# Expert blocks of a mixture-of-experts layer as pairs of 64-row sub-blocks side by side in the TensorE array, plain float32 on raw weights, row records in SBUF, two tables of sums

## Chip, cores and metric

One NeuronCore of one Trainium2 chip runs the whole program. The metric is the device time of one execution in microseconds (us). A matmul takes a stationary operand (here the transposed rows of the activations) and streams a moving operand (here the weights) past it.

## The reference, cut to what matters

`x` is 2048 rows of 1024 float32. The first half of the layer (adaLN, attention, pooling, output projection) and the router are untouched by the change in what they compute. What matters is the mixture of experts:

```
scores = sigmoid(h2 @ w_router)                      # (2048, 128)
eidx   = top 8 experts of each row (group-limited);  wts = normalised scores * 2.5
routed[t] = sum over its 8 experts e of  wts * ((silu(h2[t] @ w_gate_e[e]) * (h2[t] @ w_up_e[e])) @ w_down_e[e])
shared    = (silu(h2 @ w_sh_gate) * (h2 @ w_sh_up)) @ w_sh_down
out = rmsnorm(x1 + gate2 * (routed + shared), final_g)
# w_gate_e, w_up_e: (128, 1024, 256) float32;  w_down_e: (128, 256, 1024) float32: 3 MiB an expert
```

With the inputs given, the router sends between 26 and 410 rows to an expert, 16384 in all. In blocks of 128 rows that makes 198 blocks, and 16 more for the shared expert: 214. In sub-blocks of 64 rows it makes 315, and 32 for the shared expert: 347, or 174 pairs.

## The kernel before

**Stages.** First the conditioning vector is multiplied by `ada_w`, then a loop over 16 tiles of 128 rows does the first half of the layer and the router. It stores `x1` to `acc_tab` and `h2` to `h2_tab` in HBM, and for each routed row a record (row number, weight) into `rec_tab` in HBM, ordered by expert (eight indirect DMAs of POOL a tile, L449). Then the vector engine works out which block belongs to which expert (a chain of small instructions from L819 to L865), the tables go through HBM into one partition (`row_tab`), and the expert stage begins. A last stage reads `acc_tab`, normalises and stores `out`.

**Expert stage.** A loop over blocks of 128 rows, unrolled 8 times on each engine, run `nblk+1` times. For each block the engines do this:
- POOL (L484 to L492, and `load_rec`, L475 to L478): gather the 128 rows of `h2` of block b+4 by the indices in `rec`, an SBUF tile of 8 slots (indirect DMA, L461), scatter-add the 128 result rows of the block before into `acc_tab` (indirect DMA with add, L492), and load the records of block b+6 from HBM (L478). Before the gather it waits until all record loads issued so far have landed: `g.wait_ge(s["rec_ld"], b * 16 + 16 * (AHEAD + 2))` counts the one issued in the iteration before. Before the scatter-add it waits for the one before it (`added`).
- PE: 24 matmuls of gate and up (`parts`, L1068 to L1070, operands XR and WS), 8 transposes of the next block's rows (`transposes`, L956), 12 matmuls of down with two transposes of the hidden layer (L1097) between them. Every product is made of three: the operands are split into a high and a low part in the reduced format float32r, and high*high, high*low and low*high are summed.
- ACT: silu (L608), the high parts of rows (L590), of the hidden layer (L616) and, once per expert, of the 6144 columns of weights (`upper`, L586).
- DVE: the low parts of the same (`rows_lower`, L894; L921; `lower`, L887), the product of gate and up (L908), and the scaling of the results (L917), which waits for `added`.
- SP: the weights of an expert into one of two slots of `RAW`, in two transfers of 1 MiB for gate and up and one for down, in runs of 1 KiB per row of gate and up; a slot is free when the split has read it.

The order of the work is written out by hand and kept by semaphores; no scheduler moves anything.

## Time and profile before

| | us |
|---|---|
| median of three executions (3545.75 to 3561.34) | 3558.13 |
| span of the profiled execution, first to last instruction | 3472.9 |
| what lies around that span, against the median | 85.2 |
| expert stage in that span, first L1068 to last L1070 | 985.3 to 3417.4 |

The page's second part cuts the span into 40 slices. Its first 2 are loads and conditioning, up to about slice 11 the tile loop, from there to slice 39 the expert stage. A float32 matmul stands in the profile as two records, a float32r one or a transpose as one. The duration of a record includes its latency, so that the pitch of a run of them is found from the starts, or from (length of the run less one record) divided by (count less one).

### The profile page before, as it was taken

To read this page: it belongs to the slowest core of one execution; us is meant where nothing else is said; L and a number is where in the kernel's file an instruction comes from. 1 tells how busy PE (TensorE), PEld (TensorE's weight loads), DVE (VectorE), ACT (ScalarE), POOL (GpSimd) and SP (SyncE) were. 2 spreads that over 40 slices of the span, in tenths; PEclk is the share of its full clock that TensorE was granted. 3 is DMA by queue.
4 is the path that set the end of the run, shared out by engine and by line. 5 is a ranking of instruction groups with operands and counts; after the bars stand their busy time and mean duration, and the time that the engine had idled before them with its cause. 6 is when DMAs were issued, how large, how long until landed. Compare 5 with 4: busy or idle time off the path is not lost.

```text
span 3472.9 us, 61999 instructions
## 1 busy us (share of the span) xinstructions
PE 2951.9 (85%) x13151; PEld 2180.6 (63%) x13152; DVE 2164.1 (62%) x3443; ACT 1706.3 (49%) x2435; POOL 925.5 (27%) x794
## 2 busy tenths in 40 slices
PE   6699999999469989888798888888888888998883
PEld 2355555555358877776676767676767667776662
DVE  1146666666643665667676766666766675667774
ACT  0133333333133654656565655556556565656565
POOL 0001111111223333232333333333332323333331
PEclk9899999999779999999899999999999999999896
DMA  9501111111175887989998999899989998899997
GB/s 368 163 25 49 49 48 36 49 36 43 67 182 122 239 228 208 269 260 259 289 295 252 290 281 274 258 271 285 288 259 265 265 293 232 247 266 280 294 275 249
DMA packets 415300, 730.08 MB, mean 210 GB/s; under 512 B 31521, under 2 KB 297377, under 8 KB 414754
## 3 DMA queue, kind: packets, MB, share of 16 engines
q1 hardware_dynamic: 341314, 500.17, 42.5%
q0 software_dynamic: 73824, 228.47, 28.6%
q14 instruction: 149, 1.22, 0.1%
q8 instruction: 13, 0.21, 0.0%
HBM read 587.37 MB, written 141.19 MB: 210 GB/s over the span
## 4 chain that ended last, share of the span: by engine, by line
DMA 45%; PE 22%; issue 12%; DVE 8%; POOL 7%; POOLq 4%; ACT 2%; DVEq 0%; SPq 0%; ACTq 0%
DMA rec<-rec_tab 42%; PE PB L986 8%; POOL arena L461 3%; POOL acc_tab L492 3%; POOLq L476 3%; PE PB L951 2%; PE PB L1068 2%; PE PB L1070 2%; PE PB L1069 2%; DMA arena<-in_ada_b 1%; PE PB L1045 1%; PE PB L956 1%; DMA acc_tab<-arena,rec 1%; PE PB L970 1%; PE PB L1011 1%
## 5 line engine op out<-in xcount | busy, mean ns | idle before, releaser
L887 DVE TENSOR_TENSOR WS<-RAW,WS (+1 forms) x774 | 900.8, 1219 | 127.3 <-ACT WS L586 125.3
L586 ACT CAST WS<-RAW (+1 forms) x774 | 759.5, 1052 | 153.2 <-DMA RAW<-in_w_up_e 99.6
L1068 PE MATMUL PB<-WS,XR 128*128 x1720 | 685.6, 399 | 52.2 <-issue 46.6
L461 POOL DMA_INDIRECT arena<-h_tab,rec x219 | 255.3, 1166 | 1574.7 <-DMA rec<-rec_tab 1381.1
L1070 PE MATMUL PB<-WS,XR 128*128 x1720 | 674.7, 392 | 0.0
L1069 PE MATMUL PB<-WS,XR 128*128 x1720 | 674.0, 392 | 0.0
L917 DVE SCALAR_TENSOR_TENSOR arena<-PB,rec,G 128x512 f32<-128x512 f32 x430 | 302.5, 745 | 383.7 <-DMA acc_tab<-arena,rec 336.5
L1068 PE MATMUL PB<-WS,HR 128*128 x860 | 402.9, 468 | 154.1 <-DVE HR L921 153.0
L492 POOL DMA_INDIRECT acc_tab<-arena,rec x215 | 402.5, 1872 | 93.3 <-issue 68.4
L1068 PEld LDWEIGHTS PB<-WS,XR 128*128 128x128 f32 x1720 | 327.6, 190 | 158.7 <-issue 91.8
L1069 PEld LDWEIGHTS PB<-WS,XR 128*128 128x128 f32 x1720 | 326.7, 190 | 66.1
L1070 PEld LDWEIGHTS PB<-WS,XR 128*128 128x128 f32 x1720 | 325.4, 189 | 67.6
L1070 PE MATMUL PB<-WS,HR 128*128 x860 | 363.4, 423 | 0.0
L1069 PE MATMUL PB<-WS,HR 128*128 x860 | 361.6, 420 | 0.0
L956 PE MATMUL PB<-cst,arena 128*128 128x128 f32 x1984 | 265.4, 278 | 97.3 <-DVE arena L814 53.1
L449 POOL DMA_INDIRECT rec_tab<-recs,posi x128 | 124.6, 973 | 795.5 <-DVE recs L748 754.8
L956 PEld LDWEIGHTS PB<-cst,arena 128*128 128x128 f32 x1984 | 235.8, 143 | 138.2 <-DVE arena L814 48.4
L894 DVE TENSOR_TENSOR XR<-PB,XR 128x512 fp32r<-128x512 f32 x432 | 277.6, 684 | 65.0 <-ACT XR L590 64.8
L608 ACT ACT_TABLE_LOAD x215 | 275.8, 1283 | 74.4 <-issue 70.5
L1068 PEld LDWEIGHTS PB<-WS,HR 128*128 128x128 f32 x860 | 176.4, 205 | 193.0 <-issue 169.4
L986 PE MATMUL PB<-arena 128*128 128x512 f32 (+1 forms) x768 | 293.7, 544 | 1.5 <-ACT arena L515 1.2
L590 ACT ACTIVATE XR<-PB 128x512 fp32r<-128x512 f32 x432 | 234.6, 595 | 98.3 <-PE PB L956 98.3
(233 smaller groups left out, 2982.6 us busy)
## 6 DMA issues: line engine op xcount, KB each, us to landing
RAW<-in_w_gate_e SPq DMA_DIRECT2D x128, 1024.0 KB
RAW<-in_w_up_e SPq DMA_DIRECT2D x128, 1024.0 KB
RAW<-in_w_down_e SPq DMA_DIRECT2D x128, 1024.0 KB, 8.6
arena<-in_ada_w SPq DMA_DIRECT2D x12, 2048.0 KB, 14.3
arena<-in_x SPq DMA_DIRECT2D x32, 512.0 KB, 3.6
h_tab<-arena SPq DMA_DIRECT2D x17, 512.0 KB, 2.9
acc_tab<-arena SPq DMA_DIRECT2D x16, 512.0 KB, 2.6
out<-fa SPq DMA_DIRECT2D x16, 512.0 KB, 4.7
```

The source lines that it names most:

```text
L461: g.indirect_dma_start(xg[n % AHEAD], None, h2_tab, bass.IndirectOffsetOnAxis(ap=rec[:, n % UNROLL, 0:1], axis=0)).then_inc(s[f"xg_r{n % A ...
L492: g.indirect_dma_start(acc_tab, bass.IndirectOffsetOnAxis(ap=rec[:, (n - 1) % UNROLL, 0:1], axis=0), ys[(n - 1) % 2], None, compute_op=ALU ...
L586: nc.scalar.copy(to, of).then_inc(s["a_hig" if k < 4 else "a_hid"], 1)
L608: A_(eg, B[7][:, 0:F], ACT.Silu).then_inc(s["eg_done"], 1)
L887: last = V.tensor_tensor(lo, raw, hi, ALU.subtract)
L894: V.tensor_tensor(xl[:, 4 * n:4 * n + 4, :], B[2 + n].rearrange("p (a b) -> p a b", a=4), xhf[:, 4 * n:4 * n + 4, :], ALU.subtract).then_i ...
L917: last = V.scalar_tensor_tensor(out=ys[(n - 1) % 2][:, c * 512:(c + 1) * 512], in0=B[4 + c], scalar=recf[:, (n - 1) % UNROLL, 1:2], in1=G2 ...
L956: last = tr(B[banks[k // 4]][:, (k % 4) * P:(k % 4 + 1) * P], src[:, k * P:(k + 1) * P], ident)
L986: last = mm(B[4 + n][:, 0:w], xT[:, k, :], w_in[:, k, n * 512:n * 512 + w], start=(k == 0), stop=(k == KD - 1))
L1068: mm(bank, hi[:, k, :], w(k, 0), start=(k == 0), stop=False)
L1069: mm(bank, hi[:, k, :], w(k, EW), start=False, stop=False)
L1070: last = mm(bank, lo[:, k, :], w(k, 0), start=False, stop=(k == K - 1))
```

## The change

It does seven things together.
1. Units of two 64-row sub-blocks, A and B, replace blocks of 128 rows. A's results come out in PSUM partitions 0 to 63 and B's in 64 to 127: each matmul has a stationary operand of 128 rows by 64 columns, and A's and B's alternate. The two sub-blocks of a unit may belong to two experts. 174 units instead of 214 blocks.
2. Plain float32 matmuls on the weights as loaded. The three float32r products and the splits of weights, rows and hidden layer are gone. A reads its weights in the ring where they were loaded; for B, DVE copies gate and up (4096 columns, `gu_copy`) and ACT copies down (2048 columns, `down_copy`) of each unit to `WBG` (two buffers) and `WBD` (one).
3. A ring of four slots for weights instead of two, and loads in runs of 8 KiB per partition (`(p k)` instead of `(k p)`); the columns of `h2` and of the hidden layer are permuted to match, in the instruction that writes them (last axis stepped by 128).
4. The records of all units are read from `rec_tab` once, by four indirect DMAs, transposed by PE and kept in SBUF (`RI`, `RW`); DVE copies two columns of them a unit into `rec`. The load of records in POOL's loop is gone.
5. Two tables of sums: A adds to the first half of `acc_tab` and B to the second, which SP fills with zeros during the tile loop (16 stores of 512 KB). The last stage reads both and DVE adds them.
6. Padding rows are not gathered (an index out of bounds); they are still scattered.
7. The block tables go to one partition by 7 small matmuls instead of through HBM, and POOL clears the row buffers (128x4096) once.

The core of the diff:

```diff
-SLOTS = 2
+SLOTS = 4
+SUB = 64
@@ SP, tile loop
+                if ok(i):
+                    sp.dma_start(acc_tab[bass.ds(i * P + (T + P), P), :], zeros).then_inc(s["z_acc"], 16)
@@ SP, loads
+            def gate_up(l, e):
+                at = (l + 3) % SLOTS * EW
+                sp.dma_start(RING[:, at:at + HALF], g.rearrange("a (p k) n -> p (a k n)", p=P)).then_inc(s["w_g"], 16)
+                sp.dma_start(RING[:, at + HALF:at + GUW], u.rearrange("a (p k) n -> p (a k n)", p=P)).then_inc(s["w_u"], 16)
@@ SP, last stage
                 sp.dma_start(fa[:, lo:hi, :], acc_tab[lo * P:hi * P, :].rearrange("(t p) n -> p t n", p=P)).then_inc(s[f"f_in{n}"], 16)
+                sp.dma_start(fb[:, lo:hi, :], acc_tab[lo * P + T + P:hi * P + T + P, :].rearrange("(t p) n -> p t n", p=P)).then_inc(s[f"f_ib{n}"], 16)
@@ POOL
+            g.wait_ge(s["p_wo"], NT)
+            g.memset(arena[:, 34816:34816 + AHEAD * D], 0.0).then_inc(s["z_pool"], 1)
+            g.wait_ge(s["e_off"], 1)
+            g.wait_ge(s["st_rec"], 16 * TOPK * NT)
+            for c in range(4):
+                g.indirect_dma_start(RF[:, c].rearrange("p r a -> p (r a)"), None, rec_sub,
+                                     bass.IndirectOffsetOnAxis(ap=recb[:, c:c + 1], axis=0)).then_inc(s["e_rec"], 16)
...
                             g.wait_ge(s["xg_used"], b + 1)
-                            g.wait_ge(s["rec_ld"], b * 16 + 16 * (AHEAD + 2))
+                            g.wait_ge(s["v_rec"], b + (AHEAD + 1))
                             gather(n + AHEAD)
                             g.wait_ge(s["y_v"], b + 2)
                             g.wait_ge(s["added"], b * 16 + 32)
-                            g.indirect_dma_start(acc_tab, bass.IndirectOffsetOnAxis(ap=rec[:, (n - 1) % UNROLL, 0:1], axis=0),
-                                                 ys[(n - 1) % 2], None, compute_op=ALU.add).then_inc(s["added"], 16)
-                            load_rec(b + (AHEAD + 2), (n + AHEAD + 2) % UNROLL)
+                            g.indirect_dma_start(acc_tab, bass.IndirectOffsetOnAxis(ap=rec[:, n, 1:2], axis=0),
+                                                 ys[n % 2], None, compute_op=ALU.add).then_inc(s["added"], 16)
@@ ACT, loop
                             act.wait_ge(s["gu_done"], b + 2)
+                            silu()
+                            act.wait_ge(s["xg_used"], b + 3)
                             rows_upper()
                             act.wait_ge(s["y_done"], b + 1)
+                            hidden_T()
+                            act.wait_ge(s["w_d"], need)
+                            down_copy(RING[:, bass.ds(act.snap(at + GUW), HALF)])
@@ DVE, tile loop
-                    V.tensor_tensor(h2, h2, B2, ALU.add).then_inc(s["v_h2"], 1)
+                    V.tensor_tensor(h2.rearrange("t (k p) -> t p k", k=KD), tmpf.rearrange("t (p k) -> t p k", k=KD),
+                                    B2.rearrange("t (p k) -> t p k", k=KD), ALU.add).then_inc(s["v_h2"], 1)
@@ DVE, loop
+                            v.wait_ge(s["eg_done"], b + 2)
+                            gated()
+                            v.wait_ge(s["xg_used"], b + 3)
+                            rows_lower()
                             v.wait_ge(s["y_done"], b + 1)
                             v.wait_ge(s["added"], b * 16 + 16)
...
+                                last_ = V.scalar_tensor_tensor(out=ys[n % 2][:, c * 512:(c + 1) * 512], in0=B[4 + c], scalar=RW[:, bass.ds(b, 1)],
+                                                               in1=G2[:, c * 512:(c + 1) * 512], op0=ALU.mult, op1=ALU.mult)
...
+                            V.tensor_copy(rec[:, (n + 5) % UNROLL, :], pair[:, bass.ds(b + 5, 1), :].rearrange("p n a -> p (n a)")).then_inc(s["v_rec"], 1)
+                            v.wait_ge(s["w_g"], need)
+                            v.wait_ge(s["w_u"], need)
+                            gu_copy(n + 1, RING[:, bass.ds(at, GUW)])
@@ PE
+            def gate_up(n, wa):
+                for k in range(KD):
+                    mm(B[7][0:SUB, :], xTm[:, k, 0:SUB], wa(k), start=(k == 0), stop=(k == KD - 1))
+                    last = mm(B[7][SUB:P, :], xTm[:, k, SUB:P], WBG[n % 2][:, k], start=(k == 0), stop=(k == KD - 1))
+                last.then_inc(s["gu_done"], 1)
+            def down(c, wa):
+                for k in range(2):
+                    mm(B[4 + c][0:SUB, :], hT[:, k, 0:SUB], wa(k), start=(k == 0), stop=(k == 1))
+                    last = mm(B[4 + c][SUB:P, :], hT[:, k, SUB:P], WBD[:, k * D + c * 512:k * D + (c + 1) * 512], start=(k == 0), stop=(k == 1))
+                return last
```

Two places of the instruction order. First PE, in one iteration of the expert loop of the kernel before, from the end of gate and up to the end of down (WS are the split weights, HR the split hidden layer, cst holds the identity for transposes):

```order
L1070 MATMUL PB<-WS_50,XR_51 128x512
...
L956 MATMUL PB<-cst,arena 128x128 [waits xg_r3]
L956 MATMUL PB<-cst,arena 128x128 x7
...
L1068 REGISTER_ALU [waits v_spd]
...
L1068 MATMUL PB<-WS_50,HR_52 128x512
L1069 ISA
L1069 MATMUL PB<-WS_50,HR_52 128x512
L1070 MATMUL PB<-WS_50,HR_52 128x512
...
L1097 MATMUL PB<-cst,arena 128x128 [waits h_ready]
L1097 MATMUL PB<-cst,arena 128x128
```

The same place of the changed kernel (L1089 and L1090 are A and B of gate and up, L1096 and L1097 those of down, L977 and L1102 the transposes; the 64 is the number of PSUM partitions written):

```order
L1089 ISA [waits xgT_v,xgT_a,v_cg]
L1089 MATMUL PB<-arena 64x512
L1090 MATMUL PB<-arena 64x512
...
L977 MATMUL PB<-cst,arena 128x128 [waits xg_r3]
L977 MATMUL PB<-cst,arena 128x128 x7
...
L1096 ISA [waits a_cd,hT_a,y_v]
L1096 MATMUL PB<-arena 64x512
L1097 MATMUL PB<-arena 64x512
...
L1102 MATMUL PB<-cst,arena 128x128 [waits h_ready]
L1102 MATMUL PB<-cst,arena 128x128
```

The order of the four pieces is unchanged; the triples of full width are now pairs of half width (8 pairs for gate and up, 4 for down), and the waits on the splits (`v_spd`, `hT_sb`) are replaced by waits on the copies for B (`v_cg`, `a_cd`).

Second POOL, one iteration of its loop before:

```order
L486 ISA [waits xg_used]
L461 DMA arena<-h2_tab,rec 128x1024 [waits rec_ld]
L488 REGISTER_ALU
L490 REGISTER_ALU [waits y_v]
L492 DMA acc_tab<-arena,rec 2176x1024 [waits added]
...
L476 TENSOR_LOAD cst
...
L478 DMA rec<-rec_tab 128x2
```

And in the changed kernel:

```order
L506 REGISTER_ALU [waits xg_used]
L477 DMA arena<-h2_tab,rec 128x1024 [waits v_rec]
L508 REGISTER_ALU
L509 ISA [waits y_v]
L511 DMA acc_tab<-arena,rec 4352x1024 [waits added]
```

The gather no longer waits for a DMA that the same loop issued one iteration earlier; the scatter-add keeps its waits. The third place, DVE, one iteration of the loop of the changed kernel (before it the weights were split here once per expert, in six instructions of 1024 columns):

```order
L892 TENSOR_TENSOR arena<-arena,PB 128x128x2 [waits eg_done]
L916 REGISTER_ALU
L889 COPY arena<-PB 128x512 [waits xg_used]
L918 REGISTER_ALU
L919 ISA [waits y_done]
L922 ISA [waits added]
L922 SCALAR_TENSOR_TENSOR arena<-PB,RW_50,G2 128x512 x2
L925 ISA
L925 COPY rec<-RI_49 128x2
L886 ISA [waits w_g,w_u]
L886 COPY arena<-arena 128x4096
```

Every unit now has one copy of 4096 columns, behind the scaling, and it waits for the weights of the unit three ahead.

## Rows read from the trace of the kernel before

**Rows 1.** The page: span, and the chain that ended last.
```profile
span 3472.9 us, 61999 instructions
...
DMA rec<-rec_tab 42%; PE PB L986 8%; POOL arena L461 3%; POOL acc_tab L492 3%; POOLq L476 3%; PE PB L951 2%; PE PB L1068 2%; PE PB L1070 2%; PE PB L1069 2%; DMA arena<-in_ada_b 1%; PE PB L1045 1%; PE PB L956 1%; DMA acc_tab<-arena,rec 1%; PE PB L970 1%; PE PB L1011 1%
```
**Rows 2.** Busy time by stage; last columns TensorE clock, DMA share, GB/s.
```profile
170.00:914.00 744.00, 682.88 (x2966) 402.11 (x2964) 478.61 (x1174) 247.55 (x493) 108.68 (x112) 0.96 0.12 43
985.00:1160.00 175.00, 173.83 (x838) 142.92 (x839) 78.75 (x122) 71.09 (x106) 55.45 (x50) 0.99 0.64 163
1160.00:3417.00 2257.00, 1972.43 (x9054) 1576.38 (x9052) 1518.70 (x1936) 1326.61 (x1737) 730.38 (x591) 0.95 0.91 265
```
**Rows 3.** POOL in order of time, in the expert stage.
```profile
2318.76 0.99 POOL L461 DMA_INDIRECT arena<-h_tab,rec  x1 [8.87 <-DMA rec<-rec_tab]
2320.05 1.62 POOL L492 DMA_INDIRECT acc_tab<-arena,rec  x1 [0.30 <-issue]
2321.08 1.23 POOL L478 DMA_DIRECT2D rec<-rec_tab  x1
2330.77 0.98 POOL L461 DMA_INDIRECT arena<-h_tab,rec  x1 [8.46 <-DMA rec<-rec_tab]
```
**Rows 4.** DMA issues with median us to landing: stretch 1000 to 1160, then 3100 to 3200.
```profile
q0 software_dynamic: 5120, 16.80, 48.1%
...
acc_tab<-arena,rec POOLq DMA_INDIRECT x17, 6.7
...
acc_tab<-arena,rec POOLq DMA_INDIRECT x9, 9.4
```
**Rows 5.** PE in order of time: one block without a wait, from down to down.
```profile
3404.83 0.47 PE L1068 MATMUL PB<-WS,HR 128*128 x1
...
3413.35 1.04 PE L956 MATMUL PB<-cst,arena 128*128 128x128 f32 x8
3414.15 0.48 PE L1068 MATMUL PB<-WS,HR 128*128 x1
```
**Rows 6.** PE in order of time in the tile loop; stationary size after the operands.
```profile
500.21 1.59 PE L970 MATMUL PB<-arena 64*64 64x128 f32 x32
...
523.43 2.05 PE L1011 MATMUL PB<-arena 128*128 128x128 f32 x16 [0.65 <-ACT arena L539]
525.41 1.09 PE L1022 MATMUL PB<-arena 128*64 128x256 f32 x8
526.44 1.16 PE L1026 MATMUL PB<-arena,poolw 128*128 128x128 f32 x8
...
899.69 13.97 PE L1045 MATMUL PB<-arena 128*128 128x512 f32 x32 [1.31 <-DVE arena L767]
```
**Rows 7.** Groups by line: count, then busy us, mean ns.
```profile
L887 DVE TENSOR_TENSOR WS<-RAW,WS x768 | 893.8, 1219 | 109.8 <-ACT WS L586 107.8 <-issue 0.2
L586 ACT CAST WS<-RAW x768 | 753.6, 1052 | 106.7 <-DMA RAW<-in_w_up_e 99.6
...
L1045 PE MATMUL PB<-arena 128*128 128x512 f32 x512 | 223.5, 594 | 12.1 <-DVE arena L767 12.1
...
L917 DVE SCALAR_TENSOR_TENSOR arena<-PB,rec,G 128x512 f32<-128x512 f32 x430 | 302.5, 745 | 383.7 <-DMA acc_tab<-arena,rec 336.5 <-PE PB L1070 47.1
...
L774 DVE TENSOR_TENSOR arena<-arena,rbias 128x128 f32<-128x128 f32 x16 | 4.7, 294 | 0.6
L772 DVE TENSOR_SCALAR arena<-arena 128x128 f32<-128x128 f32 x16 | 3.5, 218 | 4.1 <-ACT arena L546 4.1
...
L435 POOL MEMSET arena<- 128x1024 int32 x1 | 1.0, 984 | 0.0
```
**Rows 8.** The hardware DMA queue in the last stage (3427 to 3473): packets, MB, share.
```profile
q1 hardware_dynamic: 4432, 16.78, 90.8%
```
**Rows 9.** Between tile loop and experts: POOL's last record store and first gather.
```profile
958.94 0.96 POOL L449 DMA_INDIRECT rec_tab<-recs,posi  x1 [0.30 <-issue]
961.98 1.00 POOL L461 DMA_INDIRECT arena<-h_tab,rec  x1 [2.08 <-DVE offi L865]
```

559 lines of the change are left out of this document (283 added, 276 removed).

## The prediction

> **What bounds the kernel now.** I read the page first. The chain that ended last is 42% loads of records from `rec_tab`, a transfer of 1 KB [rows 1]; PE's matmuls of the expert stage stand in it with 2% a line, although PE is busy 1972 us of the 2257 us between 1160 and 3417 [rows 2]. So I asked for POOL in order of time. A record load is issued at 2321.08 for 1.23 us, then POOL sits idle 8.46 us for it before it may gather; from gather to gather 12.01 us pass [rows 3]. The loop is paced by a latency: gather, scatter-add and load are issued (about 3.5 us), then the load, behind the scatter-add in the same queue, has to land. The expert stage runs from 985.3 to 3417.4, 2432 us for 215 iterations, 11.3 us each. What PE would need without waits shows in one block at the end: from 3404.83 to 3414.15, 9.32 us from down to down [rows 5]. That is 36 float32r matmuls at 0.228 and 10 transposes at 0.11. The DMA engines are the near second, 0.91 busy in that stage [rows 2]. So PE, DMA and the record chain lie within 2 us of each other, and taking away one alone would give at most 2 us a block.
>
> **The change part by part.**
>
> *PE, a unit.* A float32 record of 512 columns comes every (13.97 - 0.59) / 31 = 0.43 us [rows 6, 7], and a matmul is two of them: 0.86 us, against three float32r records, 0.68 us, before. On its own that would be dearer by a quarter. What decides is whether A and B, each 64 columns wide in the array, run at the same time. The trace has this very shape: L1022, stationary 128*64, its output first in one half of the PSUM partitions and then in the other, 8 records of 256 columns. One after another they would need 8 x 0.216 = 1.73 us until the next matmul may start; the next, L1026, starts 1.03 us after the first [rows 6]. Four steps of 0.216 make 0.86, so they ran two at a time, and 0.17 us are left over for changing the array's shape in and out. L970 says the same: 32 records of 128 columns, 3.45 us if serial, took 1.59. I therefore price a pair of matmuls at one: 0.86 us. L1026's own 8 records take 1.16 us where 8 of L1011's (16 in 2.05) would take 1.1 or less, and L1022 starts late behind L1011 by about as much, so I take 0.35 us for each change in and out, between 0.17 and 0.5.
>
> The unit has 8 pairs of gate and up (6.88), 4 pairs of down (3.44), 10 transposes at 0.11 (1.1) and two changes in and out, round the 8 transposes and round the 2 (0.7): 12.12 us. The bounds are 11.8 and 12.6. The Trainium skill, TensorEngine Tiling (Array Packing), section Key Properties, states that changing the tiling mode drains the TensorE. The trace agrees: the drain is the 0.17 us left over above; no figure stands on that page.
>
> *The expert stage.* 174 x 12.12 + 6.9 (one gate and up ahead of the loop) = 2116 us, against 2432: **-316**. The blocks get 0.8 us longer than they were, and there are 41 fewer. The whole gain is that count: 174 units against 215 iterations, since half-size sub-blocks waste fewer padding rows.
>
> *What must hide behind 12.1 us.* DVE: one product and one copy of half the width and the full width of a scaling, two scalings at 0.745, and the copy of 4096 columns. Its price is not in the trace. L887 takes 1.219 us for 1024 columns and L774 0.294 for 128, so 1.03 ns a column from two SBUF sources; L772, with one source, takes 0.218 for 128, which is about half of that a column [rows 7]. So the copy costs between 2.3 (taken) and 4.4 us, and DVE 5.1 to 7.4 us a unit. It ends before the next gate and up does; the result of the silu is then waited for only behind 8 transposes and half of down. ACT: 2048 columns at 1.03 ns (L586 [rows 7]) 2.1 us, under 5 with the rest and its table load. The single buffer for B's down is refilled while PE spends 6.9 us on gate and up. POOL: its chain is now scatter-add to scatter-add, each waiting for the one before to land: 6.7 us with the DMA engines 0.64 busy, 9.4 with them nearly full [rows 2, 4], plus 0.3. Under 12.1 in either case; the record load and its wait are off it. This is the cover for it: 2.4 us. DMA: the weights are 402.7 MB; at the rate of the last stage, 16.78 MB in 90.8% of 46 us, 402 GB/s [rows 8], they need 1002 us of all engines. Gather and scatter-add take 48.1% of 160 us for 16.80 MB, 16.5 blocks: 4.7 us a block [rows 4], 811 us for 174, less where padding is skipped. 1813 of 2116 us, 0.86; past the 16 units of the shared expert, whose weights are there, 0.90. Before it was 0.91 with two slots, and four will smooth more.
>
> *Between the stages.* POOL issued its last record store until 959.9 [rows 9]. Then come a memset of 4096 columns (4 x 0.98 [rows 7]), four record gathers at the spacing of 1.3 us, their landing, a few small copies and transposes (about 5 us), four row gathers and the first transposes. By these I reach 985, where the first matmul stood before. The table's round trip through HBM, which was waited for, is gone: **0**, between -6 and +6.
>
> *Last stage.* Twice as much is read: 8.39 MB more at 402 GB/s is 21 us. The stage was 90.8% full, so a little fits into its holes: **+18**, between +12 and +25. DVE's 16 additions at 1.2 us lie beside the loads.
>
> *Tile loop.* The 16 stores of zeros fall where the DMA share is 0.12 [rows 2]. The permuted write of `h2` has no row; it costs nothing if a stepped write runs at the speed of a plain one, and at worst doubles a 1.2 us instruction in 16 tiles, 20 us, in a loop in which PE is busy 0.92: **+3**, between 0 and +20.
>
> Sum: -316 + 0 + 18 + 3 = -295, span 3178. The profiled execution's span is 3472.9 and the median 3558.13; I carry the 85.2 us between them over unchanged and get **3263 us**. All bounds on one side would give 3193 or 3377; since they won't all fall there, the forecast's own range is 3205 to 3345.
>
> **The rivals.**
>
> *A. Pairs overlap only in part (slower, 0.08).* The gain is 295 us, or 1.70 us a unit; spread on 24 pair steps of 0.43 that is 0.07. So from a step of 0.50 on the kernel is slower. Fully serial steps give 174 x 10.3 = 1792 us more, 5055. Against it stands L1022 with four steps for eight records; for it, that L1022 is a short burst of 256 columns with no long DVE copy beside it, and that its two halves are issued one after the other, not alternating for every step. The Trainium skill, TensorE: Matmul & The Clock Gate, section Part 3, gives 2.38 for three column tiles, 0.79 of ideal; if two tiles reached 0.79, a step would be 0.54, and the time 3263 + 174 x 24 x 0.11 = 3722. By that rule; the trace has 1.73 / 0.86, the ideal 2, once the change of shape is taken off.
>
> *B. The scatter-add takes the place of the record load (0.10).* If the copy of 4096 columns keeps POOL from preparing its transfers, POOL's period is 9.4 + 0.3 + 2.3 to 4.4, that is 12.0 to 14.1 us. At the lower end it costs nothing, in the middle (13.0) 174 x 0.9 = 157, 3420; only from 13.8 on is it slower (0.02 of the 0.10). No row has such a copy beside a POOL issue. The Trainium skill, SBUF — State Buffer, describes just this as the "DVE blocks DMA" trap: a one-source float32 copy on DVE locks GpSimd out of the shared port while descriptors are to be written. Nothing in this trace shows it, as DVE's long operations here have two sources.
>
> *C. Weights come late (0.07).* At 0.90 of the DMA engines, a run of experts with under 64 rows asks 3 MiB, 7.5 us, for half a unit, 6 us. DVE's copy looks three units ahead, which eats the ring. 0.5 to 1 us a unit gives 3350 to 3437. Against it: an expert has 16 us of PE on average.
>
> *D. Better than priced (0.04).* Changes of shape that cost nothing and a step of 0.41 would give 10.9 us a unit, 3263 - 174 x 1.2 = 3054; half of that is 3160.
>
> *E. Gains and losses cancel (0.03)*, a unit at 13.8 by several small waits.
>
> **How the numbers follow.** Forecast 0.68, A 0.08, B 0.10, C 0.07, D 0.04, E 0.03. Faster by over 0.5% (about what a measurement of this kernel tells from no change): 0.68 + 0.08 + 0.07 + 0.04 = 0.87. Within 0.5%: 0.03. Slower: 0.08 + 0.02 = 0.10. The range from 3205 to 3420 leaves out A, D, E and the upper part of B, 0.2 together.
>
> **What the changed profile would show.** The expert stage lasts about 2116 us and PE passes a unit in 12.1. Two records of L1089 and L1090 start within some 0.02 us of each other and the next two 0.43 later; if they start 0.43 apart from one another, A is true. No wait on a record load remains. The scatter-add lands in under 10 us and its issue takes under 2; if the issue grows to 3 or more, B has its cause. PE's waits for DVE are those on `v_cg` (copy or weights late, C) or on `h_ready`. TensorE's clock is near 1.0 in the whole stage, where it was 0.95. The copy of 4096 columns takes 2.3 us or up to 4.4. The last stage lasts about 73 us instead of 56. I am wrong most easily in the unit: each 0.1 us in it is 17 us.

## The result, and the profile after

The changed kernel takes 3196.51 us (3194.67 to 3198.84, four executions) against 3551.94 us for the kernel before (3545.64 to 3561.34, four executions). The ratio is 0.8991, its 95% interval 0.897 to 0.9012. The forecast was 3263 us with a range from 3205 to 3420. It was right in the direction and in the length of the changed kernel's span, but 66 us too high as a time, and the time lies 8.5 us below the range. The step that failed is the last one, the 85.2 us carried over from the profiled execution to the median.

The page of the changed kernel: its span, and the chain that ended last by engine and by line.

```profile
span 3192.6 us, 48012 instructions
...
PE 65%; DMA 2%; DVE 1%; issue 0%; SPq 0%; POOL 0%; ACT 0%; DVEq 0%; POOLq 0%; ACTq 0%
PE PB L1089 37%; PE PB L1096 20%; PE PB L977 6%; PE PB L1102 2%; DMA arena<-in_w_up_e 1%; DMA arena<-acc_tab 1%; PE PB L1090 1%; DVE arena L954 0%; DVE arena L940 0%; PE PB L1097 0%; DMA acc_tab<-arena,rec 0%; DMA arena<-h_tab,rec 0%; DMA arena<-rec_tab,recb 0%; SPq L446 0%; POOL arena L488 0%
```

Where [rows 1] had 42% of the chain on the load of records, it now runs through PE's own matmuls, A's of gate and up (L1089) and A's of down (L1096). The execution took 3194.67 us and its span is 3192.6: 2.1 us lie outside the span.

The changed kernel by stage; the columns are those of [rows 2].

```profile
170.00:914.00 744.00, 661.78 (x2928) 387.60 (x2927) 477.88 (x1138) 247.20 (x493) 103.46 (x107) 0.97 0.16 54
...
1200.00:3120.00 1920.00, 1902.21 (x9192) 685.84 (x9190) 789.92 (x954) 501.12 (x636) 587.59 (x318) 1.00 0.87 282
3120.00:3193.00 73.00, 0.00 (x0) 0.00 (x0) 41.70 (x57) 31.71 (x52) 0.00 (x0) 0.50 0.87 346
```

In the expert stage PE is busy 1902 of 1920 us at a granted clock of 1.00, and the DMA engines 0.87. Of the 18 us that are left, 8.8 lie behind its end (3111.2), and 9.0 are one wait. There the weights came late. DVE's copy waited 14.08 us for them. The product of gate and up (L892) stands behind that copy in DVE's order, so it came late and kept PE waiting:

```profile
3032.09 2.29 DVE L886 COPY arena<-arena 128x4096 f32 x1 [14.08 <-DMA arena<-in_w_up_e]
...
3034.30 0.59 DVE L892 TENSOR_TENSOR arena<-arena,PB 128x256 f32<-128x256 f32 x1
...
3034.95 0.69 PE L1102 MATMUL PB<-cst,arena 128*128 128x128 f32 x2 [9.02 <-DVE arena L892]
```

PE of the changed kernel in order of time, from the end of gate and up of one unit to the start of the next one's (L1089 is A's gate and up, L1090 B's, L977 the 8 transposes of rows, L1096 and L1097 down of A and B, L1102 the 2 transposes of the hidden layer).

```profile
2302.84 0.59 PE L1089 MATMUL PB<-arena 128*64 x1
2302.85 0.59 PE L1090 MATMUL PB<-arena 128*64 128x512 f32 x1
2303.37 1.09 PE L977 MATMUL PB<-cst,arena 128*128 128x128 f32 x8
2304.39 0.64 PE L1096 MATMUL PB<-arena 128*64 x1
2304.40 0.64 PE L1097 MATMUL PB<-arena 128*64 128x512 f32 x1
...
2305.73 0.59 PE L1096 MATMUL PB<-arena 128*64 x1
...
2306.26 0.44 PE L1102 MATMUL PB<-cst,arena 128*128 128x128 f32 x2
2306.63 0.64 PE L1096 MATMUL PB<-arena 128*64 x1
...
2308.39 0.59 PE L1089 MATMUL PB<-arena 128*64 x1
2308.40 0.59 PE L1090 MATMUL PB<-arena 128*64 128x512 f32 x1
2308.82 0.59 PE L1089 MATMUL PB<-arena 128*64 x1
```

A's record and B's start 0.01 us apart, and the next two 0.43 later. So the halves of the array run at the same time, and a pair costs what one matmul costs. What the change of the array's shape costs shows in the starts: from 2302.85 to 2303.37 is 0.52 where 0.43 would do, from 2303.37 to 2304.39 is 1.02 where 8 transposes at 0.11 would need 0.88, and the first pair of down takes 0.48. In and out cost 0.09 + 0.14 + 0.05 = 0.28 us; round the 2 transposes of the hidden layer it is as much.

The costliest groups of the changed kernel.

```profile
L511 POOL DMA_INDIRECT acc_tab<-arena,rec x174 | 459.6, 2641 | 1414.0 <-DVE arena L922 1268.2
...
L886 DVE COPY arena<-arena 128x4096 f32 (+1 forms) x177 | 405.4, 2290 | 54.3 <-DMA arena<-in_w_up_e 53.3
```

POOL now waits for DVE's results (L922), which wait for PE. That is the wait of an engine with time to spare. The wait of a scatter-add for the one before it is 77.6 us in all. The copy of 4096 columns takes 2.29 us, as taken (2.3).

**The sum, term by term, in that execution.** The expert stage ran from 1001.6 to 3111.2, that is 2109.6 us, where 2116 was forecast, against 2432.1 before (985.3 to 3417.4): -322.5. It began 16.3 us later (+3 was forecast up to there). What follows it took 81.4 us against 55.5: +25.9, where +18 was forecast. The sum is -280.3 against the forecast -295, a span of 3192.6 against 3178. So the span was forecast to 0.5%. The rest of the miss is the last step, the 85.2 us.

### The profile page after: what moved, and what is told of

The parts are those of the page before. It is cut to its first block, busy times and chain, and to the rows that moved or that the text cites. A ratio compares the mean times of both kernels' runs of the same rounds, so it can differ in the third digit from the quotient of the medians.

```text
span 3192.6 us, 48012 instructions
## 1 busy us (share of the span) xinstructions
PE 2898.3 (91%) x13408; PEld 1210.9 (38%) x13409; DVE 1463.7 (46%) x2449; ACT 853.0 (27%) x1285; POOL 788.2 (25%) x493
## 4 chain that ended last, share of the span: by engine, by line
PE 65%; DMA 2%; DVE 1%; issue 0%; SPq 0%; POOL 0%; ACT 0%; DVEq 0%; POOLq 0%; ACTq 0%
PE PB L1089 37%; PE PB L1096 20%; PE PB L977 6%; PE PB L1102 2%; DMA arena<-in_w_up_e 1%; DMA arena<-acc_tab 1%; PE PB L1090 1%; DVE arena L954 0%; DVE arena L940 0%; PE PB L1097 0%; DMA acc_tab<-arena,rec 0%; DMA arena<-h_tab,rec 0%; DMA arena<-rec_tab,recb 0%; SPq L446 0%; POOL arena L488 0%
## 5 line engine op out<-in xcount | busy, mean ns | idle before, releaser
L1089 PE MATMUL PB<-arena 128*64 (+1 forms) x2800 | 1231.9, 593 | 2.1 <-issue 1.3
L1090 PE MATMUL PB<-arena 128*64 128x512 f32 x2800 | 1231.9, 593 | 0.0
L511 POOL DMA_INDIRECT acc_tab<-arena,rec x174 | 459.6, 2641 | 1414.0 <-DVE arena L922 1268.2
L1089 PEld LDWEIGHTS PB<-arena 128*64 128x64 f32 x2800 | 384.0, 137 | 802.7 <-issue 802.7
L1096 PE MATMUL PB<-arena 128*64 x1392 | 673.5, 606 | 0.0
L1097 PE MATMUL PB<-arena 128*64 128x512 f32 x1392 | 673.5, 606 | 0.0
L922 DVE SCALAR_TENSOR_TENSOR arena<-PB,RW,G 128x512 f32<-128x512 f32 x348 | 245.3, 746 | 644.2 <-PE PB L1097 610.7
L886 DVE COPY arena<-arena 128x4096 f32 (+1 forms) x177 | 405.4, 2290 | 54.3 <-DMA arena<-in_w_up_e 53.3
L1090 PEld LDWEIGHTS PB<-arena 128*64 128x64 f32 x2800 | 384.0, 137 | 0.0
L892 DVE TENSOR_TENSOR arena<-arena,PB 128x256 f32<-128x256 f32 x175 | 106.2, 607 | 546.2 <-ACT arena L594 544.5
L603 ACT COPY arena<-arena 128x2048 f32 (+1 forms) x175 | 330.9, 1891 | 0.0
L977 PE MATMUL PB<-cst,arena 128*128 128x128 f32 x1664 | 231.3, 283 | 64.5 <-DVE arena L824 36.5
L594 ACT ACTIVATE arena<-PB 128x256 f32<-128x256 f32 x175 | 67.2, 384 | 826.3 <-PE PB L1090 727.7
L977 PEld LDWEIGHTS PB<-cst,arena 128*128 128x128 f32 x1664 | 182.8, 143 | 219.6 <-issue 158.9
L1096 PEld LDWEIGHTS PB<-arena 128*64 128x64 f32 x1392 | 162.1, 136 | 257.9 <-issue 257.9
L1066 PE MATMUL PB<-arena 128*128 128x512 f32 x512 | 236.9, 623 | 9.7 <-ACT arena L571 7.0
L600 ACT ACTIVATE arena<-PB 128x256 f32<-128x256 f32 x175 | 67.2, 384 | 622.9 <-PE PB L1097 622.9
L477 POOL DMA_INDIRECT arena<-h_tab,rec x178 | 193.8, 1089 | 62.5 <-issue 54.1
L1007 PEld LDWEIGHTS PB<-arena 128*128 128x128 f32 x768 | 145.2, 191 | 131.5 <-issue 120.1
L1097 PEld LDWEIGHTS PB<-arena 128*64 128x64 f32 x1392 | 162.1, 136 | 0.0
```

What stands on the lines that cost most here:

```text
L477: g.indirect_dma_start(xg[n % AHEAD], None, h2_tab, bass.IndirectOffsetOnAxis(ap=rec[:, n % UNROLL, 0:1], axis=0), bounds_check=T - 1, oob ...
L511: g.indirect_dma_start(acc_tab, bass.IndirectOffsetOnAxis(ap=rec[:, n, 1:2], axis=0), ys[n % 2], None, compute_op=ALU.add).then_inc(s["add ...
L603: nc.scalar.copy(WBD, src).then_inc(s["a_cd"], 1)
L886: V.tensor_copy(WBGf[n % 2], src).then_inc(s["v_cg"], 1)
L922: last_ = V.scalar_tensor_tensor(out=ys[n % 2][:, c * 512:(c + 1) * 512], in0=B[4 + c], scalar=RW[:, bass.ds(b, 1)], in1=G2[:, c * 512:(c ...
L977: last = tr(B[banks[k // 4]][:, (k % 4) * P:(k % 4 + 1) * P], src[:, k * P:(k + 1) * P], ident)
```

## The experiments

**The kernel before, again.** No edit.

> The kernel before, unchanged, profiled and timed again. The forecast carried 85.2 us over that lay between the span of before's profiled execution (3472.9) and its median (3558.13); in the changed kernel only 2.1 us lie outside the span (3194.67 against 3192.6). Theory 1: the execution of before that was profiled was a fast one, and other executions have an expert stage that is longer by some 80 us, because its pace is a transfer's latency, which differs from chip to chip or from execution to execution; then the spans here follow the times to within 3 us, and where the profiled span differs from 3473 the whole difference lies in the expert stage, in the time that a record load takes to land (about 0.4 us more than the 7.7 of the first trace). Theory 2: something outside the first and last instruction costs before 85 us and the changed kernel nothing; then the profiled span is near 3473 again with a time near 3550.

3495.6 us (3490.26 to 3504.01, ten executions) beside 3499.72 in 13 more executions of the same kernel, ratio 0.9994 (0.9974 to 1.0013). The profiled execution took 3490.94 with a span of 3489.3. So there are no 85 us outside the span, only 1.6, and this kernel took some 50 us less than when it was timed first. What differed was still open.

**The record load awaited one iteration later**, in the kernel before:

```diff
-                g.dma_start(rec[:, slot, :], rec_tab[bass.ds(off, P), :]).then_inc(s["rec_ld"], 16)
+                g.dma_start(rec[:, slot, :], rec_tab[bass.ds(off, P), :]).then_inc(s[f"rec_l{slot % 2}"], 16)
-                            g.wait_ge(s["rec_ld"], b * 16 + 16 * (AHEAD + 2))
+                            g.wait_ge(s[f"rec_l{n % 2}"], (q * (UNROLL // 2) + ((n + AHEAD) // 2 + 1)) * 16)
```

> The kernel before, in which POOL waits before a gather only for the records of the block that it gathers (issued two iterations earlier, on one of two semaphores), not for the load issued one iteration earlier. Theory 1 (the record load paces the loop): the iteration falls from 11.3-11.7 us to the next bound, the DMA engines or the scatter-add that waits for the one before it (9.4 us landing and its issue), about 10.3 us, so 215 us less, near 3330. Theory 2 (the DMA engines, 0.91 busy, are the real bound and the wait only stands where they show): under 50 us less, 3500 or more.

3329.49 us (3318.51 to 3338.35), ratio 0.9533 (0.9484 to 0.9583), as theory 1 had it. POOL's wait ahead of the gather (L461), in this kernel:

```profile
L461 POOL DMA_INDIRECT arena<-h_tab,rec x219: 941/992/4492, 957.9 to 3256.7; - x110
its engine sat idle before it (us, times) until:
  issue: 70.7, 213
```

The 1381 us for which the gather waited for records are gone, and the expert stage lasts 2280 us, 10.6 us a block instead of 11.4 (2451 us) for the kernel before in the same set. The latency paced the loop, as the prediction read it, and taking it away is worth 0.8 us a block, within the 2 us that the text allowed. What paces it next is no single thing: the DMA engines are 0.96 busy from 1160 to 3256, and POOL's scatter-add now waits 845 us in all for the one before it. Half of the change's gain could be had by moving one wait. Two more sets gave 3330.08 and 3328.59, ratios 0.9528 and 0.9547.

**A copy of two columns** instead of B's 4096, in the changed kernel; B then multiplies by stale weights.

```diff
-                            gu_copy(n + 1, RING[:, bass.ds(at, GUW)])
+                            V.tensor_copy(WBGf[(n + 1) % 2][:, 0:2], RING[:, bass.ds(at, 2)]).then_inc(s["v_cg"], 1)
```

> The changed kernel with DVE's copy of 4096 columns in the loop cut to 2 columns; B of a unit then multiplies by stale weights. Theory 1 (the copy is hidden, and what it lengthens is POOL's issue of the scatter-add): time within 3 us of 3196, the issue of the scatter-add falls from a mean of 2.64 us to 1.6 to 1.9. Theory 2 (the issue is longer for another reason, such as the second table or DMA queues): the issue stays at 2.6.

3177.28 us in one execution, 19 below the changed kernel as timed first. That was not the copy. The 19 us lie ahead of the expert stage, which begins at 984.8 instead of 1001.6 and lasts 2110.5 us against 2109.6 with the copy, and the changed kernel as it is gave 3177.69 in a later set (below). So the copy costs nothing that these times show. It does show in the scatter-add's issue (L511) and its landing; here, and in that later unchanged run:

```profile
L511 POOL DMA_INDIRECT acc_tab<-arena,rec x174: 1572/1581/1626, 1011.7 to 3097.9; - x174
...
DMA to landing us min/median/max: 5.9/6.6/10.3
```

```profile
L511 POOL DMA_INDIRECT acc_tab<-arena,rec x174: 1577/2797/2807, 1008.6 to 3097.9; - x174
...
  DVE arena L922: 1337.6, 165
...
  DMA acc_tab<-arena,rec: 8.6, 1
...
DMA to landing us min/median/max: 6.4/7.8/11.9
```

The issue takes 2.80 us with the copy and 1.58 without, so rival B's cause is real, up to 1.2 us a unit. Its effect on the time is not, since POOL sat idle 1338 us for DVE's results in that run and 8.6 us for a scatter-add. With the record load put back (below), POOL's order in time shifts, and the copy falls beside the gather's issue: there the gather's takes 2.45 us (at 2299.49, the copy at 2299.53) where it takes 1.04 without the copy beside it, and the scatter-add's 1.64. The Trainium skill, SBUF — State Buffer, "SBUF: two separate sides", describes such a wait as the "DVE blocks DMA" trap (GpSimd locked out of the shared port while DVE copies float32). The trace agrees with the longer issue; no run here shows the port.

**All of A's matmuls ahead of all of B's**, in the changed kernel:

```diff
                 for k in range(KD):
                     mm(B[7][0:SUB, :], xTm[:, k, 0:SUB], wa(k), start=(k == 0), stop=(k == KD - 1))
+                for k in range(KD):
                     last = mm(B[7][SUB:P, :], xTm[:, k, SUB:P], WBG[n % 2][:, k], start=(k == 0), stop=(k == KD - 1))
```

It is the same for down.

> The changed kernel with all matmuls of A before all of B, in gate and up (8 and 8) and in each half of down (2 and 2), the same work. Theory 1 (the array runs two column halves at once only if both are near each other in PE's queue): gate and up run one after the other, 6.9 us more, the halves of down perhaps too, up to 3.4 more; a unit of 19 to 22 us, time 4400 to 5000. Theory 2 (the two halves are independent streams however they are ordered, as the 8 records of two halves in the tile loop of before suggest): still 3196.

4075.7 us in one execution, between the theories. PE of this kernel in order of time (L1089 is A's gate and up, L1091 B's):

```profile
2306.46 5.74 PE L1089 MATMUL PB<-arena 128*64 x13
2311.62 0.64 PE L1091 MATMUL PB<-arena 128*64 128x512 f32 x1
...
2312.90 0.59 PE L1089 MATMUL PB<-arena 128*64 x1
2312.95 5.74 PE L1091 MATMUL PB<-arena 128*64 128x512 f32 x13
```

Of A's 16 records 12 run alone. From the thirteenth on B's start beside them, so that 4 of B's 16 are hidden and 12 run alone. That is 28 steps instead of 16, 12 x 0.43 = 5.2 us a unit, or 898 us for 174; the difference to the span of the changed kernel in the third set (below) is 4073.6 - 3176.5 = 897. In down, with 4 records each, everything is hidden. So here a record of B started while three of A's that were issued ahead of it had yet to start, but not while more had. It is the order of issue, A and B close to each other, that makes the pair cost one.

**The changed kernel, again.** No edit.

> The changed kernel once more, unchanged, beside the others. In its first profile PE passed a tile of the tile loop every 48.7 us and the expert stage began at 1001.6 us; in the runs with a two-column copy and with A's matmuls ahead of B's, which have the same tile loop word for word, a tile took 47.2 us and the stage began at 984.8 and 982.0. Theory 1: the difference belongs to the execution, not to the kernel (another pattern of half-speed stretches of TensorE in the tile loop); then this kernel shows 3174 to 3182 here, with the expert stage beginning near 984 and lasting 2110. Theory 2: the copy of 4096 columns, or the stores of zeros, slows the tile loop; then it shows 3194 to 3199 again. The kernel before should stand between 3477 and 3561, as it has so far, and in all runs the time outside the span is about 2 us.

3197.56 us (3194.62 to 3203.03) beside 3556.56 (3534.3 to 3572.01) for the kernel before. That is theory 2's number, but not for its reason: this set ran on another chip than the four runs before it, and there both kernels stood where they had been timed first. From here on I call these times the upper band (3534 to 3572 us for the kernel before, 3195 to 3203 for the changed one), and those of the first experiments, which the changed kernel joins below with 3174 to 3179, the lower band (3477 to 3512).

**One change of shape a unit**, in the changed kernel: the 8 transposes of rows behind the first half of down, directly ahead of the 2 of the hidden layer.

```diff
-                            m = n + 2
-                            pe.wait_ge(s[f"xg_r{m % AHEAD}"], (q * (UNROLL // AHEAD) + (m // AHEAD + 1)) * 16)
-                            transposes((2, 3), xg[m % AHEAD], "xg_used")
...
                             down(0, down_a(0))
+                            m = n + 2
+                            pe.wait_ge(s[f"xg_r{m % AHEAD}"], (q * (UNROLL // AHEAD) + (m // AHEAD + 1)) * 16)
+                            transposes((2, 3), xg[m % AHEAD], "xg_used")
                             pe.wait_ge(s["h_ready"], b + 2)
                             hidden_T()
```

> In the changed kernel PE enters and leaves the shape of 128 by 64 tiles twice in a unit: round the 8 transposes of rows and round the 2 of the hidden layer. Here the 8 transposes are moved behind the first half of down, directly ahead of the 2, so that it does so once. In the trace the starts around the 8 transposes leave 0.14 us behind them, those around the 2 leave 0.15 ahead and 0.15 behind, beyond 0.43 a record pair and 0.11 a transpose. Theory 1: what is left over is the price of the change of shape and nothing hides behind it; one change in and out is 0.30 us, 174 units give 52 us less, a ratio near 0.984, and a unit of 11.7 us. Theory 2: the DMA engines, 0.87 busy in this stage, are the next bound, and weights come late for units with few rows; then under half of it shows, 0 to 25 us, with PE's waits for DVE's copy growing. Theory 3: the rows' transposes now end 1.7 us later and the copies of them keep the next gate and up waiting; 0.2 to 0.5 us a unit more, 3230 to 3280.

3147.26 us (3143.25 to 3149.73) beside 3197.56: 50.3 us less where 52 were expected. PE of this kernel in order of time:

```profile
2304.16 0.59 PE L1090 MATMUL PB<-arena 128*64 128x512 f32 x1
2304.58 0.59 PE L1096 MATMUL PB<-arena 128*64 x1
...
2305.87 0.59 PE L1097 MATMUL PB<-arena 128*64 128x512 f32 x1
2306.39 1.09 PE L977 MATMUL PB<-cst,arena 128*128 128x128 f32 x8
2307.32 0.38 PE L1102 MATMUL PB<-cst,arena 128*128 128x128 f32 x2
2307.64 0.65 PE L1096 MATMUL PB<-arena 128*64 x1
...
2309.41 0.59 PE L1090 MATMUL PB<-arena 128*64 128x512 f32 x1
```

From gate and up (2304.16) to the next one's (2309.41) it is 5.25 us, against 5.55 in the changed kernel (2302.85 to 2308.40). The stage went from 2112 to 2061 us. The rows did not come late, and the weights only in the same place as in the changed kernel (one wait of 10.2 us of PE, 10.6 there). In the set with the fourth run of the kernel before, it gave 3126.13 (3123.97 to 3129.54), ratio 0.8949 (0.8904 to 0.8994), as was expected of it there:

> The changed kernel with one change of the array's shape a unit instead of two, beside the others: 3147 beside 3197 in the upper band. In the lower band 50 us less than 3177, that is 3122 to 3132, as the saving lies in the expert stage alone.

It is the best version measured.

**A plain write of `h2`**, in the changed kernel (the experts multiply rows of the weights in another order, and in this first run the router too, so that it makes 177 units):

```diff
-                    V.tensor_tensor(h2.rearrange("t (k p) -> t p k", k=KD), tmpf.rearrange("t (p k) -> t p k", k=KD),
-                                    B2.rearrange("t (p k) -> t p k", k=KD), ALU.add).then_inc(s["v_h2"], 1)
+                    V.tensor_tensor(h2, tmpf, B2, ALU.add).then_inc(s["v_h2"], 1)
```

> The changed kernel with h2 written in plain order instead of permuted (the products of the experts are then of other rows of the weights, so the routed part is not the reference's; all sizes and counts stay the same). The stepped write took 1.94 us against 1.22 for the plain one in the kernel before. Theory 1: DVE is on the path of the tile loop there, so 16 x 0.72 = 11.5 us are gained, a ratio of 0.9964 against the unchanged one. Theory 2: PE's order covers it, as PE is 0.9 busy in the loop; within 3 us, and L740 alone is shorter.

3278.37 us (3272.59 to 3286.26), 81 more. Both theories fell. Three more units are 36 us. The rest lay in the tile loop, in which the write is an instruction of 1.2 us: most tiles took 51.4 to 54.3 us instead of 48.8, and the stage began at 1049.3 instead of 1003.4. A shorter instruction had gone with a longer loop. So the run was done again with the router's weights in plain order as well (`"(k p) n -> p k n"` in their load), which makes 174 units.

> The plain write of h2 again, with the router's weights in plain order too, so that the router sends the same rows to the same experts and there are 174 units (the run before had 177); the experts still multiply rows of the weights in another order, so the routed part is not the reference's. The first one passed a tile in 51.4 to 54.3 us against 48.8, with PE waiting up to 4.2 us ahead of the scores and its clock at half behind it. Theory 1: that is what the shorter write sets off in the order of DVE, ACT and PE, and it comes again: tiles of 51 to 54 us, 3230 to 3245. Theory 2: it was of that execution or of those data; then the expected 11 us less, a ratio of 0.9964 against the unchanged one. If the set runs where before stands in the lower band, the tile may be 47.2 us or less in both.

3172.99 us (3172.6 to 3180.81) beside 3177.69 (3173.76 to 3178.93), where the kernel before stood at 3501.54: 5 us less by the medians, with ranges that overlap, and no slow loop. Most of those 5 us do not lie in the tile loop. Its expert stage begins at 980.5, that of the changed kernel in the same set at 981.2, and the rest of the difference lies in the expert stage (2109 against 2114 us), which the write is no part of. A tile takes 47.2 us (by the starts of the second to the fourteenth), but so it does with the stepped write in the run with A's matmuls ahead of B's. Within what these runs resolve, the shorter write gains nothing. Once more, in another set, one execution gave 3180.66:

> The changed kernel with the plain write of h2 and of the router's weights (same rows to the same experts; the routed part is not the reference's). In the lower band it passed a tile in 47.0 us and gave 3173 beside 3178, a gain of 5 where 11 were expected. In the upper band, theory 1: tiles of 51 to 54 us as in the first run of the plain write there, 3230 to 3245, since that chip puts TensorE's clock down inside the tile. Theory 2: about 48.8 us or less, 3185 to 3200, and the first run owed its tiles to its other data.

The upper band did not turn up for it, so its question stays open.

**The old record load put back** into the changed kernel's loop, to a tile that nobody reads:

```diff
+            def load_spare(slot):
+                g.dma_start(spare[:, slot, :], rec_tab[slot * P:(slot + 1) * P, :]).then_inc(s["rec_ld"], 16)
...
+                            g.wait_ge(s["rec_ld"], b * 16 + 16)
                             gather(n + AHEAD)
...
+                            load_spare(n)
```

> The changed kernel with the old record load put back into POOL's loop: 1 KB from the table of records to a spare tile, issued behind the scatter-add and waited for ahead of the next gather, as before the change; nobody uses what it loads. Theory 1: the chain of gather, scatter-add, load and its landing (1.04 + 2.8 + 1.2 us of issue and 7.7 to 8.1 us until it has landed, 12.7 to 13.1 us) is longer than PE's 12.0 us a unit, so it sets the pace: 0.8 to 1.2 us a unit, 140 to 210 us more, about 3320 to 3400. The change needed the records in SBUF for its gain. Theory 2: with 174 units instead of 215 blocks and the queue shorter, the landing falls to 6 to 7 us and hides; within 20 us of the unchanged one.

3311.23 us in one execution, 114 more, with the expert stage at 2224 us, 12.8 a unit; expected were 140 to 210. The record load landed after 9.2 us in the median. The chain that ended last in this kernel:

```profile
DMA 36%; PE 19%; POOL 8%; issue 5%; POOLq 1%; DVE 1%; SPq 0%; ACT 0%; DVEq 0%; ACTq 0%
DMA spare<-rec_tab 34%; PE PB L1097 11%; PE PB L1104 6%; POOL acc_tab L517 4%; POOL arena L478 3%; PE PB L985 2%; DMA arena<-h_tab,rec 1%; DMA arena<-acc_tab 1%; PE PB L1110 1%; DVE arena L962 0%; DVE arena L948 0%; PE PB L1098 0%; POOLq L512 0%; POOLq L259 0%; POOLq L509 0%
```

Without the records in SBUF, a third of the change's gain would be lost to the same latency.

**Both kernels in a third set, and the late record wait with them.** No new edits.

> The kernel before once more, for a third profile. Its executions have stood at 3477 to 3512 us in one set of runs and at 3534 to 3572 in two others, and its first profile shows 3472.9. Theory 1: the sets ran on different chips, and the record loads land later on one of them; then this set stands in one of the two bands as a whole, and in the upper band the profile shows the same expert stage with a landing of the record load of 8.5 us or more in the median (it was 7.7 and 8.1 in the profiles of 3473 and 3489), 215 times 0.3 to 0.4 us more than the latter. Theory 2: it is chance from one execution to the next; then single executions of one set fall in both bands.

> The changed kernel in the same set. Theory 1: it has no such chain, so its expert stage lasts 2108 to 2113 us wherever it runs; if before stands in the upper band, a tile of the tile loop takes 48.8 us and the whole 3194 to 3203; if in the lower band, a tile takes 47.2 and the whole 3174 to 3182. Theory 2: the chip does not matter to it; 3194 to 3203 in either case.

> The kernel before with each record load awaited one iteration later, in the same set. It gave 3329 beside 3500 for the kernel before. Theory 1: what differs between the bands of the kernel before is the wait on the record load, so that this kernel shows 3320 to 3345 in either band, and its ratio is 0.935 if before stands in the upper one. Theory 2: everything that moves data is slower there; then it too shows 55 us more, 3385, and the ratio stays 0.953.

The kernel before gave 3498.99 (3486.87 to 3509.61), the changed one 3177.69 (3173.76 to 3178.93), ratio 0.909 (0.9052 to 0.9128), the late wait 3330.08. The lower band is the same on two chips (this one and that of the first experiments), and the changed kernel goes with it. Its stages here:

```profile
170.00:914.00 744.00, 677.59 (x2953) 399.25 (x2947) 490.14 (x1177) 248.94 (x494) 108.65 (x112) 0.96 0.16 54
...
981.00:3095.00 2114.00, 2101.12 (x10134) 757.40 (x10134) 865.28 (x1045) 551.09 (x699) 649.28 (x347) 1.00 0.82 265
3095.00:3176.00 81.00, 0.20 (x2) 0.00 (x0) 45.37 (x61) 33.88 (x54) 2.80 (x1) 0.53 0.82 317
```

It began its stage at 981.2, the kernel before in the same set at 980.8. Its span is 3176.5, and the forecast was 3178. That this is 1.5 us off is in part luck: against [rows 1] the stage gave 2 us more than forecast, what lies ahead of it 7 more, and the last stage 8 less.

**In search of the upper band.** The kernel before and the late wait in a fourth set, then the kernel before alone in a fifth. No edits.

> The kernel before a fourth time. So far sets on two chips gave 3477 to 3512 us and a set on a third 3534 to 3572, and the changed kernel went with them, 3177 and 3197, its difference of 20 us lying in the tile loop alone (47.2 to 47.5 us a tile or 48.8). No profile of this kernel in the upper band exists. Theory 1: in the upper band its tile loop takes 20 us more as well, and the expert stage the remaining 35 to 40, by record loads that land later (8.5 us or more in the median against 7.7 to 8.3). Theory 2: the expert stage is the same in both bands, and all of the 55 us lies in the tile loop or outside the span. If the set runs in the lower band, it tells nothing new but should give 3477 to 3512.

> The kernel before with each record load awaited one iteration later. On two chips it gave 3329 and 3330 beside 3500. In the upper band, theory 1 gives the tile loop's 20 us and no more, 3345 to 3355, a ratio near 0.942 to 3556; theory 2 (all transfers slower there) 3385. In the lower band 3320 to 3340 again.

> The kernel before once more, for one profile in the upper band if this set runs there. Theory 1: its tile loop takes 20 us more than in the profiles so far and its expert stage 35 to 40, with the median landing of the record load at 8.5 us or more. Theory 2: all of the 55 us lies in the tile loop. In the lower band: 3477 to 3512 once more, and the question stays open.

The fourth set was in the lower band (3487.99 and 3328.59). In the fifth the profiled execution took 3550.95 us, while the one execution beside it on the same chip took 3509.93, so that the chip alone does not decide. The stages of the kernel before in that execution, and by source line the add that writes `h2` once a tile (its first and last start stand behind the durations):

```profile
170.00:914.00 744.00, 659.01 (x2729) 389.43 (x2728) 438.90 (x1062) 235.54 (x463) 95.23 (x99) 0.93 0.12 40
914.00:1051.00 137.00, 60.49 (x276) 39.28 (x274) 77.82 (x224) 26.75 (x48) 34.06 (x35) 0.71 0.27 70
1051.00:3491.00 2440.00, 2139.86 (x9890) 1710.69 (x9890) 1595.59 (x2057) 1396.91 (x1842) 775.21 (x641) 0.96 0.90 257
```

```profile
L731 DVE TENSOR_TENSOR arena<-arena x16: 1224/1224/1226, 222.0 to 989.2; 128x1024 f32<-128x1024 f32 x16
```

The expert stage begins at 1051.3 instead of 985.3 and lasts 2439.9 us, inside what the other four profiles show (2432.1, 2451.1, 2465.9 and 2435.1). The record load lands after 8.0 us in the median, no later than elsewhere (7.7 to 8.3). Of the 76.4 us by which this span exceeds [rows 1], 66.0 lie ahead of the expert stage. Theory 2 holds for this execution: its tile loop has another pace, 54.1 us a tile from the fifth on instead of 47.5 to 47.8. In one of its tiles PE stands in order of time as follows (L1011 is the router's matmul), and below it are two stretches of 4 us of the same tile:

```profile
646.82 1.04 PE L956 MATMUL PB<-cst,arena 128*128 128x128 f32 x8
647.69 1.04 PE L1002 MATMUL PB<-cst,arena 128*128 128x128 f32 x8
652.92 3.06 PE L1011 MATMUL PB<-arena 128*128 128x128 f32 x16 [4.19 <-issue]
```

```profile
648.00:652.00 4.00, 0.73 (x7) 0.49 (x5) 0.69 (x1) 1.51 (x4) 2.90 (x3) 1.00 0.02 1
652.00:656.00 4.00, 3.08 (x18) 2.86 (x20) 0.69 (x1) 1.46 (x3) 0.00 (x0) 0.72 0.01 0
```

PE stands still for 4.19 us ahead of L1011, then its 16 records take 3.06 us where they took 2.05 in [rows 6]; the granted clock of that stretch is 0.72, a mix of its two levels, 1.2 and 2.4 GHz. In a tile of the lower band (the fourth profile) the same place looks like this:

```profile
616.33 2.05 PE L1011 MATMUL PB<-arena 128*128 128x128 f32 x16 [0.64 <-ACT arena L539]
```

The first four tiles of the slow execution stand like that too (waits of 0.64 to 0.75 us), and from the fifth on the wait is 2.8 to 4.8 us. What first makes it long, I can't tell from the trace.

## Why the prediction missed, point by point

- **The unit.** 12.12 us forecast; 12.08 measured from the first to the last scatter-add of the third set ((3097.9 - 1008.6) / 173). The pair at the price of one was exact, 0.43 a step. A change of shape in and out was priced at 0.35 us and cost 0.30 where it could be removed. The Trainium skill, TensorEngine Tiling (Array Packing), Key Properties, has the drain without a figure; here in and out together cost 0.28 to 0.30 us.
- **Rival A** would have needed a step of 0.50. The trace has 0.43 with alternating halves, twice the rate of one. An estimate from the 2.38 that the Trainium skill, TensorE: Matmul & The Clock Gate, Part 3, gives for three column tiles would have been 0.54; the trace does not bear it out for two. Rival D's step of 0.41 and free changes of shape did not come either.
- **The cover, and rival B.** The forecast named POOL's chain of scatter-adds, 9.7 us under 12.1. It held, with a longer issue (2.80) and a shorter landing (7.7 in the median) than taken. Rival B's lengthened issue came and cost nothing.
- **Rival C**, weights that come late, happened once, not in each unit. DVE waited 53.3 us in all for transfers of `in_w_up_e`, in 13 places, and 9.0 us of it reached PE, in one place (10.5 in the third set). At 11.8 us a unit, with one change of shape less, it was 10.2.
- **Where the gain comes from.** The text gave the whole of it to the count of units. That was right as a sum of two lengths and incomplete as a cause. With the record load put back, 114 of the 359 us between the two kernels of that set are lost, and taking only the wait for it out of the kernel before gains 170 us. Both were needed, because a unit of 12.0 us is shorter than what the old chain takes in it (12.8).
- **Between the stages**, 0 forecast: from the last tile's `h2` to the stage it is 63.4 us in the third set (917.8 to 981.2) and 62.3 before (923.0 to 985.3). Right, within about 1 us. The rows of the two adds, before and in the third set:

```profile
L731 DVE TENSOR_TENSOR arena<-arena x16: 1224/1225/1226, 224.8 to 923.0; 128x1024 f32<-128x1024 f32 x16
```

```profile
L740 DVE TENSOR_TENSOR arena<-arena x16: 1902/1942/1952, 220.2 to 917.8; 128x1024 f32<-128x1024 f32 x16
```

- **Last stage**, +18 forecast between +12 and +25, +25.9 and +25.8 measured in the two profiles: mis-sized. Some 2 us lie ahead of its first load (11.0 us behind the last matmul, 9.2 before), where the longer issue of the last scatter-add stands, and nothing of the 21 us fitted into the holes: the loads' queue is 90.0% full from 3128 to the end, where it was 90.8% full in [rows 8].
- **Tile loop**, +3 forecast. The stepped write takes 1.94 us against 1.22, 11.5 us in 16 tiles, and none of it showed in the time: in the third set the loop is no longer than before, and with the plain write the expert stage began less than 1 us earlier. In the upper band it takes 48.8 us a tile, 16 to 20 us more in all.
- **The step that failed** is the last: "I carry the 85.2 us between them over unchanged". The difference between the median of the timed executions and the profiled span was not a constant around the span. What lies outside the span is 2 us in every execution that has both, in both kernels. As far as the runs show, the 85.2 us set a profile of the lower band beside times of the upper one. By the profile at 3550.95 most of that is slower tile loop (66 us, and about 10 behind it), which the profiled execution did not have, and the changed kernel loses only 16 to 20 us to the upper band. The first profile was also a fast one within its band: 3472.9 is the shortest of the four spans there, and the longest, 3503.2, has 34 us more of expert stage. Compared within a band the gain, forecast as 295 us, is 321 in the lower one (3498.99 - 3177.69) and 355 to 359 in the upper one. Had I left the 85.2 out, 3180 would have stood in the text, against 3177.69 and 3196.51 measured.

That the first timed executions had the slow tile loop is concluded from their times and from the one profile at 3550.95, and not shown, since they were not profiled themselves. The granted clock over a whole execution points the same way. It is 0.932 in that profiled one, 0.929 to 0.935 in the 11 executions of the upper band in the second set, and 0.934 to 0.945 in the 69 of the lower band. Why the changed kernel, with a write that is 0.7 us longer in each tile, goes to 48.8 us a tile there and not to 54 is open: the plain write went with tiles of 51.4 to 54.3 us in the one set that might have told, but with another routing.

## What to carry to other kernels

A profiled span and a timed median may belong to two different paces of the kernel: ask where in the program their difference can lie before it is added to a forecast, and whether the change touches that place. When a loop is paced by a latency, price the removal of that wait alone before a rewrite; here it was one wait and gave half. Issue two narrow matmuls that are to share the array close to each other: 4 records ahead of 4 overlapped in full, 16 ahead of 16 only by 4. A piece of work in another shape of the array should be put next to the others of that shape; here that gave 50 us.

## What the runs showed of the hardware that was not expected

- Two float32 matmuls of 64 columns in the two halves of the array start 0.01 us apart and cost 0.43 us a record together. Issued as 16 and 16, only 4 of B's records start beside A's.
- A DVE copy of 4096 float32 columns (2.29 us) beside POOL's scatter-add goes with an issue of 2.80 instead of 1.58 us, and with a landing after 7.8 instead of 6.6 us in the median. Beside a gather it goes with 2.45 instead of 1.04 us.
- A DVE add of 1024 columns with a stepped write takes 1.94 us, with a plain one 1.22.
- The same tile loop runs at 47.5 to 47.8 or at 54.1 us a tile in different executions of one program; on one chip two executions took 3550.95 and 3509.93 us.
